# Linear attention's output layer: DMA turns rows 0 to 13, TensorE the last two, and the third k tile is computed at the layer's end

## What is computed

```
h = layer_norm(alpha * h1 + (o * silu(r)) @ w_out, g, b)      # end of the linear attention's layer
x = h[:, 16:]                                                 # the result is also kept for a later residual sum
n = x * rsqrt(mean(x * x) + eps) * pre_norm_g                 # start of the next block
q, k, v, gate, ... = split(n @ w_in)
```

## Time and profile before

| | |
|---|---|
| median of three runs | 2345.09 (2344.5 to 2346.41) |
| the profiled execution | 2344.97, its span 2343.0 |
| TensorE busy | 2264.8, 97% of the span |
| DVE, ACT, POOL busy | 62%, 48%, 37% |
| granted TensorE clock, mean | 0.986 of full |
| this stage | about 1451 to 1652 |

### The profile page before, as it was taken

The page is one execution under the profiler, slowest core; times in us unless marked ns, Lnnn a source line. Parts: engine busy times, 40 slices in busy tenths (PEclk is TensorE's granted clock), DMA queues, the critical chain, the costliest instruction groups (busy, mean ns, idle before and its releaser), DMA issues. The chain is left out here.

```text
span 2343.0 us, 35223 instructions
## 1 busy us (share of the span) xinstructions
PE 2264.8 (97%) x13534; PEld 1165.1 (50%) x13534; DVE 1458.6 (62%) x2401; ACT 1124.1 (48%) x2179; POOL 876.7 (37%) x673
## 2 busy tenths in 40 slices
PE   8999999998998999999999998999999999999998
PEld 4555555543444445454454554444655555444443
DVE  6999999977555245545445446678377776245323
ACT  7766666686763334334344334333266665333211
POOL 2988888878895111111102010444033333000000
PEclk9999999999999999999999999999999999999999
DMA  5011110033334400100000012223200000102232
GB/s 210 28 45 46 46 46 24 28 119 124 125 119 157 90 2 6 55 1 23 37 1 6 1 55 81 82 90 108 73 10 14 16 1 1 41 19 97 74 108 90
DMA packets 54301, 134.71 MB, mean 57 GB/s; under 512 B 5423, under 2 KB 25519, under 8 KB 53112
## 3 DMA queue, kind: packets, MB, share of 16 engines
q1 hardware_dynamic: 54136, 132.46, 17.1%
HBM read 96.65 MB, written 35.80 MB: 57 GB/s over the span
## 5 line engine op out<-in xcount | busy, mean ns | idle before, releaser
L1178 DVE SCALAR_TENSOR_TENSOR cv_tap_sum<-cv_glu,cv_prm,cv_tap_sum 128x1024 f32<-128x1024 f32 x326 | 418.9, 1288 | 11.9 <-ACT cv_tap_sum L666 2.4
L931 POOL TENSOR_TENSOR mixed<-mixed,cv_tap_products 128x1024 f32<-128x1024 f32 x153 | 363.9, 2379 | 78.0 <-ACT cv_tap_products L681 62.5
L100 PE MATMUL cv_proj<-H_hi,cv_w_ga 128*128 128x416 f16 (+1 forms) x640 | 217.2, 339 | 8.2 <-DVE H_lo L1151 8.2
L101 PE MATMUL cv_proj<-H_lo,cv_w_ga 128*128 128x416 f16 (+1 forms) x640 | 217.3, 339 | 0.0
L102 PE MATMUL cv_proj<-H_hi,cv_w_ga 128*128 128x416 f16 (+1 forms) x640 | 217.2, 339 | 0.0
L100 PE MATMUL gm_vr<-gm_wvr_hi,H_hi 128*128 128x512 f16 x512 | 195.1, 381 | 0.0
L101 PE MATMUL gm_vr<-gm_wvr_lo,H_hi 128*128 128x512 f16 x512 | 195.1, 381 | 0.0
L102 PE MATMUL gm_vr<-gm_wvr_hi,H_lo 128*128 128x512 f16 x512 | 195.1, 381 | 0.0
L1860 POOL TENSOR_TENSOR gm_q_inter<-gm_q_rel,gm_block_decays 128x512 f32<-128x512 f32 x16 | 16.7, 1047 | 453.5 <-ACT gm_block_decays L1942 417.6
L681 ACT ACTIVATE cv_tap_products<-cv_glu,cv_prm 128x1024 f32<-128x1024 f32 x138 | 151.6, 1138 | 35.5 <-POOL mixed L931 35.4
L2470 POOL TENSOR_TENSOR at_probs<-at_probs,at_rsum 128x768 f32<-128x768 f32 (+1 forms) x64 | 90.3, 1411 | 165.3 <-DVE at_rsum L2754 165.3
(11 more groups left out here) (461 smaller groups left out, 5718.2 us busy)
## 6 DMA issues: line engine op xcount, KB each, us to landing
cv_w_stage<-conv_w SPq DMA_DIRECT2D x24, 512.0 KB, 3.9
mixed<-gla_w SPq DMA_DIRECT2D x8, 1024.0 KB, 7.8
go_rows<-h_rows SPq DMA_DIRECT2D x16, 512.0 KB, 4.0
h_rows<-go_rows SPq DMA_DIRECT2D x16, 512.0 KB, 2.8
pl_sums_a<-h_rows SPq DMA_DIRECT2D x16, 512.0 KB, 3.5
out<-pl_sums_a SPq DMA_DIRECT2D x16, 512.0 KB, 2.6
cv_tap_products<-gate_z SPq DMA_DIRECT2D x24, 256.0 KB, 4.7
mixed<-xT SPq DMA_DIRECT2D x12, 416.0 KB, 8.6
```

The source lines that it names most:

```text
L100: nc.tensor.matmul(out, w_hi, x_hi, start=first, stop=False)
L101: nc.tensor.matmul(out, w_hi, x_lo, start=False, stop=False)
L931: nc.gpsimd.tensor_tensor(c_unit(U), c_unit(U), prod[:, r % 3, :], ALU.add).then_inc(s_add, 1)
L1178: nc.vector.scalar_tensor_tensor(out=acc_unit(U), in0=window(U, k), scalar=col(U // 2, k), in1=acc_unit(U), op0=ALU.mult, op1=ALU.add).the ...
```

## The change

DVE's result `normed` of rows 0 to 13 (DIRECT = 14) is split into halves before it is turned: ACT copies it to fp16 (`normed_hi`), POOL subtracts (`normed_lo`), and SP issues two DMA transposes, one into H_hi and one into H_lo. The last two rows still go through TensorE, with two PSUM banks instead of four. The two banks that this frees become `lead`, which now lives through both stages: the third k tile is computed into it at the end of `gla_out`, and `attn_mix` uses it as `p_scores`. The sum of squares gets a scratch buffer of its own. The k tiles now also wait for the DMA transposes of their rows.

```diff
+        squares = m.sb("squares", [P, D], F16)
+        halves = [m.sb("normed_hi", [P, 2, D], F16), m.sb("normed_lo", [P, 2, D], F16)]
+        DIRECT = NR - 2
...
-        pt = [[m.ps(f"tr{b}{h}", [P, 512]) for h in range(2)] for b in range(2)]
+        pt = [m.ps(f"tr{h}", [P, 512]) for h in range(2)]
...
+        def turned(s):
+            return 32 * (s // 2 + 1)
...
+                def turn_row(s):
+                    if s == 0:
+                        sp.wait_ge(s_wl, 2 * KT)
+                    for H, x, done in ((H_hi, halves[0], s_th), (H_lo, halves[1], s_tl)):
+                        sp.wait_ge(done, s + 1)
+                        sp.dma_start_transpose(H[:, :, META + s * P:META + (s + 1) * P], x[:, s % 2]).then_inc(s_tr[s % 2], 16)
...
                     if 4 <= s + 1 < NR:
                         load_row(s + 1)
+                    if s >= 2:
+                        turn_row(s - 2)
                     if s == NR - 3:
...
+                def low(s):
+                    if s >= 2:
+                        pool.wait_ge(s_tr[s % 2], turned(s - 2))
+                    pool.wait_ge(s_th, s + 1)
+                    nc.gpsimd.tensor_tensor(halves[1][:, s % 2], hn[:, s % 2], halves[0][:, s % 2], ALU.subtract).then_inc(s_tl, 1)
...
                     nc.gpsimd.tensor_tensor(tile(s), tile(s), b_bc[:, :], ALU.add).then_inc(s_h, 1)
+                    if 1 <= s <= DIRECT:
+                        low(s - 1)
...
                     wait_h(act, s)
-                    if s >= 2:
-                        act.wait_ge(s_tr, 2 * (s - 2) + 2)
-                    nc.scalar.activation(hn[:, b], tile(s), ACT.Square, accum_out=s2[:, b, 0:1]).then_inc(s_sq, 1)
+                    nc.scalar.activation(squares[:, :], tile(s), ACT.Square, accum_out=s2[:, b, 0:1]).then_inc(s_sq, 1)
...
                 def high(s):
-                    for h in range(2):
-                        act.wait_ge(s_tr, 2 * s + h + 1)
-                        nc.scalar.activation(columns(H_hi, s, h), turned(s, h), ACT.Copy).then_inc(s_th, 1)
+                    if s < DIRECT:
+                        if s >= 2:
+                            act.wait_ge(s_tr[s % 2], turned(s - 2))
+                        act.wait_ge(s_hn, 2 * s + 2)
+                        nc.scalar.activation(halves[0][:, s % 2], hn[:, s % 2], ACT.Copy).then_inc(s_th, 1)
+                    else:
...
                 def next_k(T):
                     pe.wait_ge(s_kl, 1)
-                    pe.wait_ge(s_t, 2 * (END - 1) + T + 1)
+                    for b in range(2):
+                        pe.wait_ge(s_tr[b], turned(4 * T + 2 + b))
+                    if T < 2:
+                        pe.wait_ge(s_t, 2 * (END - 1) + T + 1)
...
                     if s >= NR:
                         next_k(s - NR)
-                    if s >= 2:
+                    if s == NR + 1:
+                        next_k(2)
+                    if s >= NR:
                         transposes(s - 2)
...
                     dve.wait_ge(s_vec, 16 * 3)
+                    if s >= 2:
+                        dve.wait_ge(s_th, s - 1)
+                        dve.wait_ge(s_tl, s - 1)
...
-                    if s >= 2:
+                    if s >= NR:
                         low(s - 2)
...
-                for T in range(2, NBLK // 4):
+                for T in range(3, NBLK // 4):
```

More of the change, by code:

```diff
@@ L1325, in _, with gla_out @@
                             nc.vector.tensor_tensor(tile(LAST)[:, c], tile(LAST)[:, c], b_bc[:, c], ALU.add).then_inc(s_lh, 1)
-def gla_out(nc, ahead, next_loads, rows_in, vecs, rows_out, pre_g, gs, early_w, front, M, H_hi, H_lo):
+def gla_out(nc, ahead, next_loads, rows_in, vecs, rows_out, pre_g, gs, early_w, front, lead, M, H_hi, H_lo):
     g_dram, b_dram = vecs
@@ L1461, in high @@
                 def high(s):
-                    for h in range(2):
-                        act.wait_ge(s_tr, 2 * s + h + 1)
-                        nc.scalar.activation(columns(H_hi, s, h), turned(s, h), ACT.Copy).then_inc(s_th, 1)
+                    if s < DIRECT:
[4 more added lines that the diff above has]
+                    else:
+                        for h in range(2):
+                            act.wait_ge(s_lt, 2 * (s - DIRECT) + h + 1)
+                            nc.scalar.activation(columns(H_hi, s, h), last_turned(h), ACT.Copy).then_inc(s_lth, 1)
                 for s in range(NR + 2):
@@ L1481, in next_k @@
                     pe.wait_ge(s_kl, 1)
-                    pe.wait_ge(s_t, 2 * (END - 1) + T + 1)
+                    for b in range(2):
+                        pe.wait_ge(s_tr[b], turned(4 * T + 2 + b))
+                    if T < 2:
+                        pe.wait_ge(s_t, 2 * (END - 1) + T + 1)
                     for k in range(KT):
-                        mm = three_pass(nc, po[0][T], wkv[0][:, 0, k, :], wkv[1][:, 0, k, :], H_hi[:, k, token_tile(T)],
+                        mm = three_pass(nc, po[0][T] if T < 2 else lead[:, 0, :], wkv[0][:, 0, k, :], wkv[1][:, 0, k, :], H_hi[:, k, token_tile(T)],
                                         H_lo[:, k, token_tile(T)], k == 0, k == KT - 1)
@@ L1564, in low @@
                     for h in range(2):
[L1565 to L1566 removed]
+                        dve.wait_ge(s_lth, 2 * (s - DIRECT) + h + 1)
+                        nc.vector.tensor_tensor(columns(H_lo, s, h), last_turned(h), columns(H_hi, s, h), ALU.subtract).then_inc(s_ltl, 1)
                 for s in range(NR + 2):
@@ L2362, in pool_piece, with attn_mix @@
     return w[:, 4 * h:4 * h + 4, :].rearrange("p k n -> p (k n)")
-def attn_mix(nc, ahead, next_w, w_tiles, sink, copies, early_w, front, M, H_hi, H_lo):
+def attn_mix(nc, ahead, next_w, w_tiles, sink, copies, early_w, front, lead, M, H_hi, H_lo):
     with ExitStack() as ctx:
@@ L2393, in attn_mix @@
         p_q, p_g = front[:, 0, :], front[:, 1, :]
-        p_s, p_t = m.ps("p_scores", [P, 2, 512]), m.ps("p_probsT", [P, 2, 512])
+        p_s, p_t = lead, m.ps("p_probsT", [P, 2, 512])
         p_ot = [m.ps(f"p_oT{b}", [P, 512]) for b in range(2)]
@@ L3212, in program @@
         front = ctx.enter_context(nc.psum_tensor("front", [P, 2, 512], F32))
-        gla_out(nc, ahead, attn_first_loads(M, w_kv, w_attn), h1, (ln_g[1:2], ln_b[1:2]), h2, pre_g, gain,
-                early_w, front, M, H_hi, H_lo)
-        attn_mix(nc, ahead, w_pool[0], w_attn, sink, copies, early_w, front, M, H_hi, H_lo)
+        with ExitStack() as two:
+            lead = two.enter_context(nc.psum_tensor("lead", [P, 2, 512], F32))
+            gla_out(nc, ahead, attn_first_loads(M, w_kv, w_attn), h1, (ln_g[1:2], ln_b[1:2]), h2, pre_g, gain,
+                    early_w, front, lead, M, H_hi, H_lo)
+            attn_mix(nc, ahead, w_pool[0], w_attn, sink, copies, early_w, front, lead, M, H_hi, H_lo)
         pool_final(nc, ahead, w_pool, pool_w, pool_scale, edges, w_out, post_g, h2, out, early_w, front, M, H_hi, H_lo)
```

23 lines of the change are left out of this document (13 added, 10 removed).

## The result

The change makes the kernel faster: 2331.64 us median of four runs (2329.3 to 2332.71) against 2344.80 of four runs of before in the same series, ratio 0.9946 with a 95% interval of 0.9929 to 0.9963. Forecast were 2336.0 and faster with a chance of 0.72. The ratios are estimates from all executions of a series, not the quotients of the two medians; one execution of before in the second series, of 4774.17 us, is left out of them.

A forecast was written before the change was run, and what follows sets the result against it. TensorE, busy for 97% of the span, was taken to bound the kernel. Of 12.2 us removed, 3.1 comes back as waits for the chain: 2345.1 - 9.1 = 2336.0 us, range 2331 to 2349.

The forecast's parts named there:

- Transposes removed, 12.2: Row loop on TensorE: transposes of rows 0 to 13 go, 14 x 0.87 = 12.2 us less work.
- What is late next: Row loop: the chain DVE, ACT, POOL, DVE of 10.47 a row sets the pace; row 14's second sum 9.1 earlier.
- ACT's copy and DVE's lost subtractions, nothing: Row loop: DVE's 28 subtractions go, ACT gets one 1.04 us copy per row; both counted at nothing.
- POOL's subtraction: Row loop on POOL: one added subtraction per row, 2.3 us, free by 1.3 us a row.
- Rival 2: Row loop: POOL's subtraction holds up DVE's statistics and sums, rows up to 12.8, +20 us, 2360; chance 4%.
- The DMA transposes: SP's queue: 28 transposes of 256 KB at 3.2 us each, issue 0.6; 9.6 of 10.47 a row, hidden, 8% reserve.
- rival 1: SP's queue: transposes too slow, ACT's copies wait for them; 2395 at 8 us each, 2820 at 25.6; chance 14%.
- When too slow, how dear: SP's queue: transpose pace T per row decides from 11.05; from 11.8 nothing is gained, through ACT's waiting copies.
- Rival 3: Queue and stage's end: weights or transposes late by a few us, 2341 to 2349, no measurable difference; chance 9%.
- Weights tight, 0 to 1 us late: Next k weights, loaded behind row 11's transposes: landed by 1621 at most, ACT may start at 1620.5; taken as 0.
- The stage's end: TensorE after the row loop: idle 2.2 before tile 0 and 1.9 after; v projection at 1654.75 instead of 1663.82.
- Rival 4: Stage's end: TensorE's shorter stops (2.2, 1.9) leave the clock at 2.4 GHz, saving 2.0, 2334; chance 15%, within faster.

The follow-up runs named there:

- e9: Kernel before, all rows turned by TensorE, only ACT's and DVE's order changed (second norm of the previous row first, row 14 normalized earlier): 2336.77 us, ratio 0.9973.
- e7: Changed kernel with ACT's second norm of the previous row first and DVE normalizing row 14 ahead of the last row's gain and bias: 2326.72 us, ratio 0.9938.
- e2: Changed kernel with all 16 rows turned by TensorE again, keeping two PSUM banks and the moved third k tile: 2341.86 us, ratio 1.0000 to before.
- e3: Changed kernel with POOL's multiplication and addition on 8 of 1024 columns in rows 0 to 14, output not the layer's: 2329.25 us, ratio 0.9941.
- e4: Changed kernel with each DMA transpose issued twice (2332.81 us, ratio 0.9966) or three times (2343.22 us, ratio 1.0003).
- e1: Changed kernel with the third k tile back in the next stage: 2328.96 us, ratio 0.9941 to before.
- e5: Changed kernel with the third k tile placed ahead of row 14's transposes instead of row 15's: 2326.66 us, ratio 0.9936 to before.
- e0: Changed kernel run once more, unaltered, as yardstick in a second series: 2334.06 us against 2340.83 before, ratio 0.9961.
- e8: Changed kernel with the new ACT and DVE order and also the third k tile ahead of row 14's transposes: 2325.63 us, ratio 0.9925 to before.

## Why the prediction was right, point by point

- **Transposes removed, 12.2.** Right: 12.06 between e9 and e7, and in e2, where only the turning is undone, the gain is gone.
- **The total.** The stage was 0.55 better than forecast. The median was 4.4 lower than the 2336.0; that it stayed inside the range by 0.6 is in part luck, as it hangs on how the executions fell into the two groups.
- **What is late next.** Right in kind and nearly in size: a chain of 10.42 where 10.47 was taken. Over the 12 rows it makes the 0.6 by which row 14 came earlier than forecast (135.52 against 136.1), and with it all of the 0.55 by which the stage did. e3 and e7 show that it is this chain, and that POOL's pair beside L1600 makes it so long.
- **ACT's copy and DVE's lost subtractions, nothing.** Right: the copy took 1.06 and waited 4.46 for DVE.
- **POOL's subtraction.** 2.13, forecast 2.3, and free by 1.34, forecast 1.3. Rival 2 is out: statistics of 675 ns beside it, and a residual sum of 0.69 in e7.
- **The DMA transposes.** The term that was mis-sized, in both directions. Of the queue a transpose took 1.4 us instead of the 3.2 taken, and of SP's issue 1.24 instead of 0.6. The first made the reserve not 8% but 43% (two transposes and the rows' traffic, 2 x 1.4 + 3.1 = 5.9 of 10.42), which e4 confirms: twice is free. Packets of 256 B took 22 ns and not the 50 of the 1 KB packets in the earlier trace rows, so the choice of that row set the price too high; the count of 1024 per transpose was right. It changed nothing in the sum; what it made too dear is rival 1, with its 14%.
- **The rule on the transposes' rate.** After's DMA rows give 0.262 MB in 1.4 us, 187 GB/s, against 339 for the rows' own traffic. The Trainium skill, Advanced Engine Details and Errata, section X-Bar Transpose (TRN2), has them about as fast as ordinary ones; here they ran at some 55% of that, which leaves the sum as it is. The Trainium skill's page DMA: Bandwidth & Descriptors, by whose table rival 1 had an extreme of 27 us on SP, is not borne out: SP was held for 1.24 us, and 3.91 at most behind the weights. (The 1.2 GHz in that estimate is not a figure of the page it names.)
- **When too slow, how dear.** Not tested by the change but by e4: the prediction let the cost set in at T = 11.05 and reach the gain at 11.8, by ACT's copies waiting for transposes. At T = 11.6 the whole gain was gone already and 3.8 more, and no copy waited. The mechanism of rival 1 was the wrong one: the row loads and the k weights behind the transposes are late sooner. Rival 3 had the weights, and its 2341 to 2349 covers what e4 gave with three (2343.22).
- **Weights tight, 0 to 1 us late.** They were issued at 1603.16 and took 4.4 to 8.5 us to landing, so the last was there by about 1613.2; ACT came to them in its own order at 1614.81, without a wait. They were not late.
- **The stage's end.** Right in total, 23.46 from row 14's transposes to V, forecast 23.4. Inside it, tile 0 did not start slowly (1.5 forecast), which only turned into a longer wait for row 14's normalizing, 3.19 instead of 1.9. The transposes and tile 1 took 7.87 (8.0), the boundary 3.55 (3.5), tile 3 6.86 (6.65). Rival 4 held for the first stop (1.56, clock kept) and not for the second, which had grown to 3.19 and is the one that costs.
- **Tile 2 moved, nothing.** Right as work (e1, e2), but for a clock that fell or not at the boundary, 1.5 to 1.7 us with either place of the tile. What the prediction did not see is that placed one step earlier it wins 3.4 us and the clock with it (e5).
- **The rest of the median.** Another 0.64 us came after V (679.18 before, 678.54 after). e2 and e5 have the low figure as well, e9 and e4 three times the high one (679.27, 679.15). No run isolates it, and it stays open. With the stage's 9.62 that makes -10.3 which the traces place. The two profiled executions of after differ by 3.5 us, all of it before R1, at clocks of 0.987 and 0.989; that the same holds between the groups of executions, and so between -10.3 and the medians' -13.2 and -6.8, is likely but not shown, as only one execution of each series was profiled.

## What to carry to other kernels

When work is taken from the engine that bounds a loop, time the next chain around the loop first: it decided here how much of 12.2 us arrived (9.6). What it lacked was only order: running DVE's two-operand work before POOL's pair instead of beside it gave 6.9 more, of which 4.5 is to be had without the change too (e9) and 2.4 is what the chain had kept back. Move a filler tile to the place where the wait is, not to the place where its operands first allow it. And price a DMA queue by what stands behind it: at a pace 11% too slow it was the row loads and the next stage's weights, not the transposes' own readers, that lost the whole gain.

## What the runs showed of the hardware that was not expected

- A DMA transpose of 128 x 1024 fp16 within SBUF is cheap on this chip: 1.24 us of SP, 1024 packets, 1.4 us of the 16 engines, 3.1 us to landing, and four per row hide behind 10.4 us of matmuls.
- DVE's L1600, two operands in SBUF beside the scalar, takes 1.42 for two alone and 4.13 when POOL's multiplication and addition run beside it (e3, e7 against after), while the residual sum, which reads PSUM (0.69 in e7), and the statistics (675 ns) do not change beside POOL's subtraction. The split of the weights (L1623 in e7), with two SBUF operands as well, took 2.56 beside POOL and 1.21 without it.
- The same stop of TensorE at the stage boundary, 2.49 to 2.60 us, lowered the granted clock in before, after, e0, e3, both e4, e7, e8 and e9, and not in e1, e2 and e5; it costs 1.5 to 1.7 us. Waits of 1.5 before tile 0 never did; those of 2.4, 2.95 and 3.19 before row 14's transposes did, and so did one of 2.00 in e4 with three (eight transposes in 1.52), where TensorE had stood for 14.55 shortly before. What decides between them is open.
